# A two-direction recurrence kernel: one 128-row seed product, a straight TensorE program, and another order of work at the operand exchange

## The reference, cut to what matters

```
diff = b_c[:, :, :, None, :] - b_c[:, :, None, :, :]      # cumulative log decay, per channel
a = einsum('bhid,bhjd,bhijd->bhij', q_c, k_c, masked_exp(diff, incl))
o = einsum('bhck,bhkv->bhcv', qd_c, s) + einsum('bhij,bhjv->bhiv', a, v_c)
s = fl_c[..., None] * s + einsum('bhck,bhcv->bhkv', kd_c, v_c)
```

```
x = x + gate1 * (concat(gdn, hgrn) @ w_out)
h = modulate(rms_norm(x), shift2, scale2)
out = rms_norm(x + gate2 * (relu(h @ w1) ** 2 @ w2))
```

## Time and profile before

| what | us |
|---|---|
| three runs | 3826.36, 3834.29 (median), 3836.73 |
| the profiled execution | 3824.62, span 3822.8 |
| projections | 110 to 1060 of the span |
| GDN scans | 1075 to 1720 |
| HGRN context and chunk stage | 1720 to 2180 |
| states and merge | 2180 to 2352 |
| out phase | 2352 to 3823 |
| PE busy over the span | 3359.1 (88%) |
| DVE, POOL, ACT busy | 1987.7, 1679.2, 1644.8 |

### The profile page before, as it was taken

How to read it: one execution, slowest core, us unless ns; L and a number is a source line. 1 busy time by engine, 2 the same in 40 slices (tenths; PEclk the granted TensorE clock), 3 DMA queues, 4 the chain that set the end, 5 groups by cost and what they waited for, 6 DMA issues and landing times. The chain is left out here.

```text
span 3822.8 us, 99139 instructions
## 1 busy us (share of the span) xinstructions
PE 3359.1 (88%) x41449; PEld 2778.1 (73%) x41449; DVE 1987.7 (52%) x2884; ACT 1644.8 (43%) x2375; POOL 1679.2 (44%) x1364
## 2 busy tenths in 40 slices
PE   6899999999968888885777665999999999999998
PEld 3677888888857777774766524877878887787877
DVE  5488411110035555554555567565555556667575
ACT  5566413433135555551433423564454444323243
POOL 0211222332035454532555327546555665565564
PEclk8899999999979999996777767999999999999999
DMA  5133533453233333324433265666664657645453
GB/s 197 48 69 72 103 99 121 140 139 104 68 100 106 105 104 107 104 92 117 110 97 94 94 212 204 220 234 201 201 230 167 200 194 275 228 162 226 176 220 121
DMA packets 438928, 560.20 MB, mean 147 GB/s; under 512 B 119852, under 2 KB 355728, under 8 KB 413720
## 3 DMA queue, kind: packets, MB, share of 16 engines
q1 hardware_dynamic: 412512, 518.30, 42.3%
q10 hardware_dynamic: 20536, 21.58, 1.7%
q0 software_dynamic: 5632, 16.78, 1.5%
HBM read 354.42 MB, written 202.16 MB: 146 GB/s over the span
## 5 line engine op out<-in xcount | busy, mean ns | idle before, releaser
L2970 PE MATMUL o_pg<-o_t_hi,o_s_hi 128*128 128x512 f32 x2016 | 794.4, 394 | 54.9 <-ACT o_part L3017 18.2
L2972 PE MATMUL o_pg<-o_t_lo,o_s_hi 128*128 128x512 f32 x2016 | 790.4, 392 | 0.0
L2973 PE MATMUL o_pg<-o_t_hi,o_s_lo 128*128 128x512 f32 x2016 | 790.1, 392 | 0.0
L601 PE MATMUL p_pg<-h_hi,p_whi 128*128 128x512 f32 (+1 forms) x1384 | 531.5, 384 | 9.6 <-DVE p_wlo L830 9.6
L601 PE MATMUL p_pg<-h_hi,p_wlo 128*128 128x512 f32 (+1 forms) x1384 | 519.3, 375 | 0.0
L601 PE MATMUL p_pg<-h_lo,p_whi 128*128 128x512 f32 (+1 forms) x1384 | 519.2, 375 | 0.0
L2970 PEld LDWEIGHTS o_pg<-o_t_hi,o_s_hi 128*128 128x128 f32 x2016 | 381.9, 189 | 144.6 <-issue 37.4
L2973 PEld LDWEIGHTS o_pg<-o_t_hi,o_s_lo 128*128 128x128 f32 x2016 | 382.0, 189 | 80.7
L2972 PEld LDWEIGHTS o_pg<-o_t_lo,o_s_hi 128*128 128x128 f32 x2016 | 382.4, 190 | 78.7
L3167 DVE TENSOR_TENSOR o_s_lo<-o_raw,o_s_hi 128x512 fp32r<-128x512 f32 x288 | 262.6, 912 | 199.3 <-ACT o_s_hi L3006 199.1
L601 PEld LDWEIGHTS p_pg<-h_hi,p_whi 128*128 128x128 f32 x1384 | 262.4, 190 | 61.1 <-DVE p_wlo L830 9.8
(11 more groups left out here) (332 smaller groups left out, 6691.2 us busy)
## 6 DMA issues: line engine op xcount, KB each, us to landing
o_raw<-in_w_mlp SPq DMA_DIRECT2D x32, 1024.0 KB, 6.0
scr_f<-o_xf SPq DMA_DIRECT2D x64, 512.0 KB, 7.8
o_raw<-scr_f SPq DMA_DIRECT2D x32, 1024.0 KB, 5.3
scr_w<-o_pre SPq DMA_DIRECT2D x16, 1792.0 KB, 6.8
o_t_raw<-scr_w SPq DMA_DIRECT2D x28, 1024.0 KB, 5.4
g_kqvb<-scr_kqv SPq DMA_DIRECT2D x72, 384.0 KB, 3.5
o_xf<-scr_x SPq DMA_DIRECT2D x22, 1024.0 KB, 7.9
p_raw<-in_w_in SPq DMA_DIRECT2D x38, 512.0 KB, 6.0
```

Of the source, the lines that this page charges most:

```text
L601: last = nc.tensor.matmul(pg[0:m, bank, 0:n], w[:, q, k, 0:m], h[bank][:, k, :], start=(k == 0 and j == 0), stop=(k == KT - 1 and j == 2))
L2970: nc.tensor.matmul(out, s_hi[:, q, k, :], t_hi[:, q, k, :], start=(not more and k == 0), stop=False, skip_group_check=more)
L2972: nc.tensor.matmul(out, s_hi[:, q, k, :], t_lo[:, q, k, :], start=False, stop=False, skip_group_check=more)
L2973: last = nc.tensor.matmul(out, s_lo[:, q, k, :], t_hi[:, q, k, :], start=False, stop=(k == 3), skip_group_check=more)
```

## The change

1. **Seed.** Both directions are one batch of 16 matmuls over all 128 partitions. For that the key copy `km` now also holds the forward keys in `lo` (one more ACT copy of 64x1024 ahead of `km_first`), and the query must stand unreversed in both halves. So SP loads the `hi` half from the same memory as the `lo` half, the reversed memory copy `shqr` is given up with the ACT, DVE and DMA work that made it in the projection stage, and DVE's first product of query and decay (L2173, 128x1024) becomes two of 64 partitions, the second of which reads the query reversed.
2. **PE's program straight.** Bodies 0 to 8 of the chunk stage are written out on PE; DVE, ACT, POOL and SP keep their loops.
3. **Exchange.** `t_low` stands at other steps, and ahead of `s_low`; in an exchange's steps ACT does `t_high`, then `s_high`, then `f_unit`, where `f_unit` was first and `t_high` last; the `s` parts come earlier (`LATE_PREP`), `raw_load` a step later. Around units 7 to 10 `roots` and `scale` of the last two `h` units come earlier, `take_h` of the last one, its join and its store later.

```diff
@@ PE head, chunk stage
-                    pe.wait_ge(k_in[g][p], got(i, m, 32))
+                    pe.wait_ge(km_first[g], at(i, m, 1, 1))
                     pe.wait_ge(q_in[g][p], got(i, m, 32))
                     head_space(pe, g, i, m, a_seed, o_taken)
                     for h in range(HEADS):
                         for x in (lo, hi):
-                            last = nc.tensor.matmul(px[x, 0, h, :], ks[g][p][lo, h, x], qb[g][p][lo, h, x], start=(h == 0), stop=False)
-                    last.then_inc(seed_f[g], 1)
-                    pe.wait_ge(seed_f[g], at(i, m, 1, 1))
-                    pe.wait_ge(km_first[g], at(i, m, 1, 1))
-                    for h in range(HEADS):
-                        for x in (lo, hi):
-                            last = nc.tensor.matmul(px[x, 0, h, :], km[g][p][hi, h, x], qb[g][p][hi, h, ::-1][:, x], start=False,
-                                                    stop=(h == HEADS - 1))
-                    last.then_inc(seed_b[g], 1)
+                            last = nc.tensor.matmul(px[x, 0, h, :], km[g][p][:, h, x], qb[g][p][:, h, x], start=True, stop=True)
+                    last.then_inc(seed[g], 1)
@@ PE
-                steps(pe, first, body)
+                first()
+                for j in range(NP + 1):
+                    body(None, j, j < NP, j > 0, j < NP - 1)
@@ ACT keys
                     act.wait_ge(k_in[g][m % 2], got(i, m, 32))
+                    nc.scalar.activation(km[g][m % 2][lo], ks[g][m % 2][lo], ACT.Copy)
                     nc.scalar.activation(km[g][m % 2][hi], ks[g][m % 2][hi, :, ::-1], ACT.Copy).then_inc(km_first[g], 1)
@@ DVE head
-                    dve.tensor_tensor(qp[g][p][:, :, :], qb[g][p][:, :, :], fb[g][p][:, :, :], ALU.mult).then_inc(q_first[g], 1)
+                    dve.tensor_tensor(qp[g][p][lo], qb[g][p][lo], fb[g][p][lo], ALU.mult)
+                    dve.tensor_tensor(qp[g][p][hi], qb[g][p][hi, :, ::-1], fb[g][p][hi], ALU.mult).then_inc(q_first[g], 1)
@@ out phase
-T_HIGH, T_LOW = 2, 3
-LATE_PREP = ((), (), (), (0,), (1, 2), (3, 4), (5, 6))
+T_HIGH = (2, 3, 4, 5, 6, 7, 8)
+T_LOW = (3, 4, 5, 6, 8, 9, 10)
+LATE_PREP = {3: (0, 1), 4: (2, 3), 5: (4, 5), 6: (6,)}
@@ out phase, SP
-                        if q == (5 if last else 1 if first else 0) and i + 2 < N:
+                        if q == (6 if last else 2 if first else 0) and i + 2 < N:
                             raw_load(i + 2)
@@ out phase, ACT
-                            if not is_x(i):
+                            if not is_x(i) and q == 2:
                                 f_unit(i, q)
-                        for at in prepared(i, q):
-                            s_high(*at)
+                        if M1 - 2 <= i - 1 < M1:
+                            if q == 2:
+                                roots(i - 1)
+                            if q == 3:
+                                scale(i - 1)
                         if exchange(i, q, T_HIGH):
                             t_high(*exchange(i, q, T_HIGH))
+                            for at in prepared(i, q):
+                                s_high(*at)
+                        if 0 <= i < N and not is_x(i) and q > 2:
+                            f_unit(i, q)
+                        if not exchange(i, q, T_HIGH):
+                            for at in prepared(i, q):
+                                s_high(*at)
...
-                        if i - 1 == M1 and 2 <= q <= 3:
-                            take_h(i - 2, q - 2)
+                        if i - 1 == M1 and q >= 5:
+                            take_h(i - 2, q - 5)
@@ out phase, DVE
+                        if exchange(i, q, T_LOW):
+                            t_low(*exchange(i, q, T_LOW))
                         for at in prepared(i, q):
                             s_low(*at)
-                        if exchange(i, q, T_LOW):
-                            t_low(*exchange(i, q, T_LOW))
```

More of the change, by code:

```diff
@@ L503, in walk @@
                 b.group += n * TILES
-                b.out += 16 * TILES // 2 * {"hq": 2, "hff": 4, "hfb": 4}.get(kind, 1)
+                b.out += 16 * TILES // 2 * {"hff": 4, "hfb": 4}.get(kind, 1)
                 b.ready += TILES // 2
@@ L507, in walk @@
                     b.par += TILES
-                if kind in ("hq", "hff", "hfb"):
-                    b.mul += 2 * TILES
+                b.mul += {"hq": TILES, "hff": 2 * TILES, "hfb": 2 * TILES}.get(kind, 0)
                 b.acty += n * TILES
@@ L789, in one_kind @@
                                 if j == 0:
-                                    per = 16 * {"hq": 2, "hff": 4, "hfb": 4}.get(kind, 1)
+                                    per = 16 * {"hff": 4, "hfb": 4}.get(kind, 1)
                                     act.wait_ge(y_out[u], i * per + b.out)
-                                    if kind in ("hq", "hff", "hfb"):
+                                    if kind in ("hff", "hfb"):
                                         act.wait_ge(y_out[1 - u], i * per + (b.out + u * per))
@@ L811, in one_kind @@
                                     last = nc.scalar.activation(put(srow), src, ACT.Sigmoid, scale=-1.0)
-                                if kind == "hq":
-                                    last = nc.scalar.activation(put(srow, True), src, f)
                                 last.then_inc(group_free, 1)
@@ L1713, in q_free @@
                     if again(i, m):
-                        sp.wait_ge(seed_b[g], at(i, m, 1, -1))
+                        sp.wait_ge(seed[g], at(i, m, 1, -1))
                         sp.sem_inc(load_go, 1)
@@ L2404 @@
 MIXED = {4: 0, 1: 1, 6: 2}
-PRE_AT = [71 + 13 * t for t in range(7)] + [171 + 13 * t for t in range(8)] + [281]
+PRE_AT = [75 + 12 * t for t in range(7)] + [171 + 13 * t for t in range(8)] + [281]
 PRE_PIECES = {3: (0, 1), 4: (2,), 5: (3, 4), 6: (5, 6), 7: (7,)}
 PRE_STORE = 9
-T_HIGH, T_LOW = 2, 3
-LATE_PREP = ((), (), (), (0,), (1, 2), (3, 4), (5, 6))
+T_HIGH = (2, 3, 4, 5, 6, 7, 8)
+T_LOW = (3, 4, 5, 6, 8, 9, 10)
+LATE_PREP = {3: (0, 1), 4: (2, 3), 5: (4, 5), 6: (6,)}
 def join_operands(eng, t, done, count):
@@ L2696, in prepared, with join_due @@
             if i - 1 in LAST_OF:
-                return [(i + 1, p) for p in LATE_PREP[q]]
+                return [(i + 1, p) for p in LATE_PREP.get(q, ())]
             return [(i + 1, q)] if i + 1 < N else []
+        def join_due(i, q):
+            for j in (i - 2, i - 3):
+                step = 7 * i + q - (7 * (j + 2) + {M1 - 2: 4, M1 - 1: 7}.get(j, 0))
+                if 0 <= j < M1 and 0 <= step < 3:
+                    return j, step
+            return None
         def is_x(i):
@@ L2738, in quarter, with exchange @@
             return t.rearrange("p (u j) -> p u j", j=P)
-        def exchange(i, q, lag):
-            at = 7 * i + q - lag
-            i, q = divmod(at, 7)
-            return (LAST_OF[i], q) if i in LAST_OF else None
+        def exchange(i, q, at):
+            for last in (i, i - 1):
+                if last in LAST_OF and 7 * (i - last) + q in at:
+                    return LAST_OF[last], at.index(7 * (i - last) + q)
+            return None
         with nc.Block() as block:
@@ L2853, in _ @@
                             h_store(i - 2)
-                        if q == 0 and M1 - 2 <= i - 3 < M1:
+                        if q == 0 and i - 3 == M1 - 2 or q == 3 and i - 3 == M1 - 1:
                             h_store(i - 3)
@@ L3109, in _ @@
                                 squares(i - 1)
-                            if q == 2:
+                            if q == 2 and not M1 - 2 <= i - 1 < M1:
                                 roots(i - 1)
                         if 0 <= i - 1 < M1:
-                            if q == 3:
+                            if q == 3 and i - 1 < M1 - 2:
                                 scale(i - 1)
```

46 lines of the change are left out of this document (19 added, 27 removed).

## The result

The changed kernel takes 3787.9 us (median of three, 3783.71 to 3791.86) against 3834.29 before: the ratio is 0.988, with an interval of 0.9865 to 0.9898. The forecast was 3790. The total came out as forecast, but not its parts. Of the 42 us of the sum 18 were to come from the heads, 9 from the jumps and 15 from the exchanges.

What follows compares the result with a forecast made beforehand. PE was taken to bound projections and undisturbed out-phase units, no engine the chunk stage. Heads 18, jumps 9 and exchanges 15 make 42 off the 3834.29 median, 3792, put at 3790; forecast range 3775 to 3797 (0.52).

Steps and rivals of the forecast that it cites:

- the sum: Whole kernel: heads 18, jumps 9 and exchanges 15 add to 42 us saved.
- the heads: Chunk stage: one seed batch instead of two saves PE 22.3, less 4 for DVE: 18 us, bounds 10 to 25.
- the jumps: Chunk stage: straight PE program removes two loop jumps costing 10.6 us; 9 taken, bounds 0 and 11.
- the exchanges: Out phase: new order saves 3 at units 48 to 64, 4 at 24 to 41, 8 at 7 to 10: 15 us.
- Projections, 0: Projection stage: dropping the reversed copy's ACT, DVE and store work gains 0, since PE fills the stretch.
- no loss hides here: Dropped reversed copy: without PE's cover its removal would be a gain, so the 0 conceals no loss.
- I leave the other issue waits where they are: Chunk stage: straight code removes only the jumps' waits; PE's other "issue" waits stay, as body 7's 6.1 us showed.
- DVE eats the head's gain: Rival, chance 0.13: DVE's full 12 us loss and ACT's copy cut the heads from 18 to 4; 3804 us.
- The DVE result serves one lane while PE works on the other: Chunk-stage heads: reason to charge only a third, 4 us, of DVE's possible 11 to 12 us loss.
- ACT's copy: Chunk-stage heads: added key copy, 1.04 us per head, 15 us over 14, hidden because ACT is busy 160.14 of 410.00.
- the lower bound: Chunk-stage heads: least gain, 22.3 - 12 = 10 us, said to include ACT's copy without its cover.
- Slower: Rival, chance 0.03: late 1 MB loads hold back ACT's in-order work at the exchanges; 3846 us or more.

Runs made afterwards that it cites:

- x1: Kernel before with only the one-batch seed and the dropped reversed query copy, PE's loop and exchange as before: 3802.1 us, ratio 0.992.
- x4: Changed kernel with the out phase of before, so new seed and straight PE program together: 3794.3 us, ratio 0.9904.
- x2: Kernel before with only PE's chunk program written out straight: 3809.5 us, ratio 0.9943.
- x7: Changed kernel with DVE's first query-decay product as one 128-partition operation again, backward query's reversal left out: 3773.3 us, ratio 0.9848.
- x8: x7 with ACT's two key copies also made one of 128 partitions, backward keys' reversal left out: 3771.6 us, ratio 0.9853.
- x12: Changed kernel with four idle semaphore increments on SP ahead of its GDN scan loop; SP's branch step 0.244 us, GDN scans within 653.1 to 665.9.
- x9: Changed kernel with two idle semaphore increments on SP ahead of its GDN scan loop; SP's branch step 0.099 us, GDN scans within 641.7 to 650.9.

## Why the prediction was right, and where it was not

**The sum** held: 42 forecast for a gain of 46.4 between the medians. It held by luck, since two errors met: terms that were too large by 8.5 together (27 forecast for 23.5 and 15 for 10), and 11 us from a place that it had called 0.

**Projections, 0**: right, PE filled the stretch as before. But "0" was said of the whole dropped copy. Without its two stores in SP's program the loop of the next stage stood elsewhere. The step that failed is the "0" for the whole copy, since nothing was asked about the stage behind; "no loss hides here" held, it was a gain that hid.

**Jumps, 9 of 10.6**: the term was mis-sized where it stands alone: it was worth 22 in time (16 to 27) and 25 in the stage. Beside the new seed (x1 to x4) it was 11 in the stage, close to the 9. DVE's idle time ahead of the first instruction of a body, from which it was sized, holds only the first of the waits that a jump leaves behind. The bodies with the jumps were 8 and 10 longer than in x2, and the rest of the 25 lies in the other bodies, on which I have no experiment of its own. The step "I leave the other issue waits where they are" held: 38.7 to 54.8 us of them stand in the ten kernels with a straight program, and 37 to 53 outside the jumps in the three with the old chunk stage. The Trainium skill's page "Runtime: NRT & Kernel Launch", section "Instruction fetch mechanics", says that a taken branch whose target is outside the window forces a fetch and a stall, and these traces agree (12.2 us at two jumps). Its "mostly hidden" for the crossings of straight code holds only in part here: the waits come 256 instructions apart, at 29 of 78 places over 0.3 us in the changed kernel, and add up to 38.7 us of 388.

**Heads, 18**: the mechanism was there and the price of a batch near (25.1 against 27.3). Alone the seed gave 12 in the stage. Beside the straight program it gave 0 (386.3 and 387.5), and the step that failed is the addition of the two. The rival "DVE eats the head's gain" is what happened: I charged 4 for DVE's second product, x7 shows 11. The rows that told it were there: DVE's wait of 1.01 and the 2.8 against it. Behind the 14 heads these waits are now under 0.1 in eleven places and at most 0.87, so DVE is late at nearly all of them, not at half. "The DVE result serves one lane while PE works on the other" gave no relief; that DVE serves both lanes, and that POOL's operations beside the products became longer by 12 us in all, are two explanations that no run tells apart. ACT's copy, "hidden" in the sum, may cost another 4 to 5 by x8's stage, which x8's time doesn't confirm. It was not in the lower bound either, as the text had it: 22.3 - 12 = 10 holds DVE's cost alone.

**Chunk stage in all**: 27 forecast, 23.5 on average (410.9 to 387.4) over the first two sets. How it falls to the two parts depends on the order: 12 for the seed and then 11 for the jumps, or 25 for the jumps and then nothing for the seed.

**Exchanges, 15**: the sizes were too large, the order of the terms right. The excess over 19.04 per unit, averaged over the five kernels with the old and the five with the new order in the first two sets, fell from 88.5 to 78.5 in the whole out phase, 10. Units 7 to 10 gave 6.5 (8 forecast), units 24, 25, 40 and 41 gave 3.0 (4), the three at 48, 56 and 64 gave 1.9 (3). Against them the undisturbed units among 11 to 47 lost 1.4. For the last exchanges the row that was wrong is the price of a `t_low` and an `s_low` in company: 2.76 and 1.75 for 2.29 and 0.69. With these the new wait three products on takes back all that the first gives (4.89 for 4.82), and what gain there is came with the granted clock, which the sum for unit 48 didn't have. For the second the copy L3017 came sooner and PE's stall fell from 6.36 us in the trace of before to 3.53, but the unit behind, at 21.43, was longer than before (20.82), and at the next such exchange unit 41 took 23.20 for 20.77, at a clock of 0.93 for 1.00.

**Slower**: not in the sum of any exchange, but in single units. The longest is unit 8, 28.97 for 26.74, where PE's wait for the copy L3017 grew from 1.79 to 3.46 and the clock fell from 1.00 to 0.88; it gave back less than units 9 and 10 gained. Whether late 1 MB loads are behind it, as the rival had it, was not looked into.

## What to carry to other kernels

Two savings on one chain don't add: cost each with the other already made, and ask which engine's wait is then the shortest. A fixed 1.23 us of DVE per head was worth 11 us of stage beside the straight program. Run the code that you did not change several times too: "issue" waits of one and the same chunk stage read 38.7 and 51.5 in two traces, and one trace against one would have told a story about them. When operations go from an engine that runs a loop later, measure the later loop too, and measure an unchanged stage before calling a term right: the total alone would have confirmed a sum whose parts were off by up to a factor of two. Where an engine with a hardware loop feeds the critical path at the top of each turn, try a few idle instructions ahead of it, as x12 and x9 did, or (not tried here for SP) the loop written out.

## What was not expected of the hardware

- The step over a loop's branch depends on where the loop lies in the engine's program. On SP it was 0.244 us, and 0.107 with two stores (four instructions) fewer ahead; with two of the four put back 0.099, with all four 0.244. On ACT it was 0.214 and 0.091, and ten idle instructions brought 0.214 back. Over 33 turns SP's step is only 4.5 us; the scans lost 11. The gap between the stores and the load, 0.75 against 0.54, gives 7 of it; POOL's waits for that load show 10.4, and why they grow by more than the gap was not followed.
- PE's issue waits in straight code stand 256 instructions apart: 29 of 31 in the changed kernel, 35 of 36 in x2.
- The 64-partition product with a reversed read took 1.22 us on DVE each time, the one of 128 partitions 1.21 to 1.23 in 14 of 16 cases and 2.1 in the two others (mean 1.33 before).
- With two DVE products POOL's 240 operations of the chunk stage took 242 to 246 us in seven kernels; with one product 227 to 230 in the seven others, whichever seed they had. Two thirds of it are in the 16 operations that stand beside the products: 16.6 us before, 28.3 after, 18.9 in x7.
- Units with the same waits, 4.9 us in all, took 24.8, 26.0 to 26.4 or 27.2 us at a granted clock of 1.00, 0.94 or 0.88.
